# Modulation sums of a diffusion block: from column sums on TensorE to accumulating VectorE operations, with the first projection done block by block

## The reference, cut to what matters

```python
D_MODEL, SEQ, DEPTH, MOD_CHUNKS, SGU_WIDTH, N_MIXERS = 1024, 256, 2, 6, 2048, 3
for i in range(DEPTH):                      # layer 0: gMLP mixer, layer 1: pooling mixer
    mod_lat = split((silu(c) @ ada_w[i] + ada_b[i])[:, None, :], MOD_CHUNKS, axis=-1)   # ada_w[i]: 1024 x 6144
    h_lat = rmsnorm(x_lat, norm1_g[i]) * (1 + mod_lat[1]) + mod_lat[0]
    y_lat = mixer(h_lat)                    # layer 0: z = gelu(h @ w_in); v half normed, mixed over tokens, times u; @ w_out
    x_lat = x_lat + mod_lat[2] * y_lat
    f_in = rmsnorm(x_lat, norm2_g[i]) * (1 + mod_lat[4]) + mod_lat[3]
    x_lat = x_lat + mod_lat[5] * peer(f_in) # product-key expert retrieval over 16,384 experts, tables u and v
out = rmsnorm(x_lat, final_gain)
```

## Time and profile before

| | |
|---|---|
| timed runs | 1875.08, 1877.49, 1878.11 us; median 1877.49 |
| the profiled execution: span from first to last instruction | 1874.9 us |
| median of the timed runs less this span | 2.6 us |
| TensorE busy | 1853.5 us, 99% |
| VectorE busy | 1530.4 us, 82% |
| ScalarE busy | 956.6 us, 51% |
| GpSimd busy | 409.0 us, 22% |
| moved by DMA | 376.38 MB, mean 201 GB/s |

### The profile page before, as it was taken

One profiled execution on the slowest core, in us unless ns is written; L12 is line 12 of the kernel. 1 busy time (PEld: TensorE's weight loads), 2 busy tenths in 40 slices (PEclk: granted clock), 3 DMA queues, 4 the chain that ended last, 5 costly groups with the idle time before them and its releaser, 6 DMA issues.

```text
span 1874.9 us, 35845 instructions
## 1 busy us (share of the span) xinstructions
PE 1853.5 (99%) x11924; PEld 1599.7 (85%) x11924; DVE 1530.4 (82%) x2739; ACT 956.6 (51%) x1588; POOL 409.0 (22%) x197
## 2 busy tenths in 40 slices
PE   7999999999999999999999999999999999999998
PEld 6899998888888888888889998888888888888887
DVE  7785689978988888888887588997998888885555
ACT  3644455655555544445455445565555544445454
POOL 1015578970000000000001258895000000000000
PEclk9999999999999999999999999999999999999999
DMA  9956455556645555578874445556654555555554
GB/s 363 331 204 215 146 171 188 184 185 218 209 167 169 178 170 177 170 284 319 327 280 165 140 160 188 182 188 202 208 207 160 173 173 177 169 175 191 193 190 134
DMA packets 104180, 376.38 MB, mean 201 GB/s; under 512 B 12464, under 2 KB 12464, under 8 KB 103856
## 3 DMA queue, kind: packets, MB, share of 16 engines
q1 hardware_dynamic: 103680, 373.43, 58.6%
q0 software_dynamic: 432, 2.10, 0.3%
HBM read 374.43 MB, written 1.05 MB: 200 GB/s over the span
## 4 chain that ended last, share of the span: by engine, by line
PE 93%; DVE 3%; DMA 2%; ACT 1%; SPq 1%; issue 0%; DVEq 0%; ACTq 0%
PE ring L1708 22%; PE O L1766 13%; PE O L1768 12%; PE O L1767 12%; PE ring L1710 11%; PE ring L1409 3%; PE ring L1410 3%; PE ring L1411 3%; PE ring L1680 3%; PE ring L1701 2%; DMA raw<-in_u 1%; PE O L1701 1%; PE ring L1682 1%; DMA raw<-in_w_in 1%; PE O L1512 1%; PE O L1555 1%
## 5 line engine op out<-in xcount | busy, mean ns | idle before, releaser
L489 ACT ACTIVATE wH<-raw 128x1024 fp32r<-128x1024 f32 x606 | 643.3, 1062 | 833.6 <-DMA raw<-in_v 366.0
L1708 PE MATMUL ring<-hX,wH 128*128 128x512 f32 x1984 | 703.6, 398 | 0.0
L807 DVE TENSOR_TENSOR wL<-raw,wH 128x1024 fp32r<-128x1024 f32 x384 | 470.2, 1224 | 178.7 <-ACT wH L489 175.4
L1710 PE MATMUL ring<-hX,wL 128*128 128x256 f32 x1984 | 554.8, 280 | 0.0
L1708 PEld LDWEIGHTS ring<-hX,wH 128*128 128x128 f32 x1984 | 372.4, 188 | 86.0 <-issue 0.5
L1766 PE MATMUL O<-wH,gateH 128*128 128x512 f32 x1024 | 405.3, 396 | 0.0
L1768 PE MATMUL O<-wH,gateL 128*128 128x512 f32 x1024 | 399.5, 390 | 0.0
L1767 PE MATMUL O<-wL,gateH 128*128 128x512 f32 x1024 | 398.3, 389 | 0.0
L1710 PEld LDWEIGHTS ring<-hX,wL 128*128 128x128 f32 x1984 | 374.4, 189 | 0.0
L452 POOL TENSOR_TENSOR wL<-raw,wH 128x1024 fp32r<-128x1024 f32 x128 | 318.3, 2493 | 53.0 <-ACT wH L489 52.0
L1768 PEld LDWEIGHTS O<-wH,gateL 128*128 128x128 f32 x1024 | 192.2, 188 | 41.2
(11 more groups left out here) (205 smaller groups left out, 2353.7 us busy)
## 6 DMA issues: line engine op xcount, KB each, us to landing
raw<-in_u SPq DMA_DIRECT2D x256, 512.0 KB, 3.3
raw<-in_v SPq DMA_DIRECT2D x256, 512.0 KB, 3.3
ada_v<-in_ada SPq DMA_DIRECT2D x40, 512.0 KB, 4.5
raw<-in_w_in SPq DMA_DIRECT2D x32, 512.0 KB, 4.6
raw<-in_w_q SPq DMA_DIRECT2D x30, 512.0 KB, 3.3
ada_s<-in_ada SPq DMA_DIRECT2D x20, 512.0 KB, 5.2
ada_f<-in_ada SPq DMA_DIRECT2D x16, 512.0 KB, 9.9
raw<-in_w_out SPq DMA_DIRECT2D x16, 512.0 KB, 3.3
```

The source lines that it names most:

```text
L489: nc.scalar.activation(wH[s % RAW][:, :], (place or raw[s % RAW])[:, :], ACT.Copy).then_inc(s_h, 1)
L807: nc.vector.tensor_tensor(wL[s % RAW][:, :], raw[s % RAW][:, :], wH[s % RAW][:, :].bitcast(fp32), ALU.subtract).then_inc(s_low, 1)
L1708: mm(bank[:, :], wH[s][:, k * P:k * P + P], hX[:, k, :, :].rearrange("p two t -> p (two t)"), start=(k == 0), stop=False)
L1710: ins = mm(bank[:, 0:T], wL[s][:, k * P:k * P + P], hH[:, k, :], start=False, stop=(k == KT - 1))
```

## The change

- The host now gives `ada_w` transposed: an ada tile holds 128 output columns on the partitions and all 1,024 rows along the free side. Tile m gives `mod[:, m]` in one VectorE operation: tile times the condition row, with `accum_out` taking the sum along the free side. The row (silu(c) on every partition, 128 x 1024) is made once by 8 matmuls of a broadcast column of csT against the identity into PSUM banks O[2] and O[3], and ScalarE copies it to SBUF as `cond`. In front and in w_out the operation reads the row from PSUM (`O23`, refilled by ScalarE ahead of w_out), elsewhere from SBUF.
- All `modulations` matmuls of TensorE go. In the second norms, and in layer 0's last norm, keep_clock matmuls stand where they stood.
- Front: SyncE loads XT first, then for each pair of k blocks four ada tiles (two of chunk 1, two of chunk 0) mixed with three gate tiles. VectorE sums the two tiles of block k, makes gs and shift for that block, and scales and shifts the block of XT (normed beforehand into `sq`). TensorE takes each block as it comes, in groups 0 to 2 (1,536 columns, six banks), and does group 3 behind them in the last two banks. GpSimd makes the low parts of these twelve tiles in halves, VectorE those of the last four.
- w_out: the low part of all 16 tiles is made by GpSimd, whole.
- Ada tiles: none in w_v beyond the sixteen of the front, 12 loads in w_u (8 of them summed there), 12 loads and 16 sums in w_out (OUT_ADA says how many before each low part's old place: 1, 1, 1, 1, 2, 1, 2, 1, 1, 1, 1, 1, 1, 1, 0, 0); u and v as before, the v loop of VectorE written out.

```diff
@@ SyncE
+            sp.dma_start(XT[:, :, :], xt_d).then_inc(s_x, 16)
+            for g in range(4):
+                if g == 0:
+                    load(stream_dram["w_v", 0], 0, 0, 0, first=True)
+                load_front(4 * g)
+                load_front(4 * g + 1)
+                if g == 0:
+                    load(stream_dram["w_v", 0], 0, 0, 1, first=True)
+                else:
+                    load_gate(3 * g)
+                    load_gate(3 * g + 1)
+                load_front(4 * g + 2)
+                load_front(4 * g + 3)
+                load_gate(3 * g + 2)
+            for t in range(BLOCK_TILES, 16):
+                load_gate(t)
             for dst, src in small_loads:
                 sp.dma_start(dst, src).then_inc(s_small, 16)
...
                 load(stream_dram["w_u", 0], W_U, t // 4, t % 4)
-                if t < 8:
-                    load_ada(ada_s, m)
+                if t < 8 or t > 11:
+                    load_ada(ada_m, m)
                     m += 1
...
                 load(stream_dram["w_out", 0], W_OUT, t // 4, t % 4)
-                if t in ADA_W_OUT:
-                    if t == ADA_W_OUT[0]:
-                        sp.wait_ge(s_gf, SGU_FT)
-                    load_ada(ada_o, m)
+                if 2 < t < 15:
+                    load_ada(ada_m, m)
                     m += 1
@@ GpSimd
-                    low_second(W_OUT, 0, 0, W_OUT + 1)
+                    for t in range(BLOCK_TILES):
+                        front_low(t)
+                    low_out(0, 0, W_OUT + 1)
@@ ScalarE, ahead of w_out
                     gated_high(15, 16)
                     act.wait_ge(s_small, SMALL)
+                    act.wait_ge(s_sv, SGU_FT)
+                    for x in range(2):
+                        nc.scalar.activation(O[2 + x][:, :], cond[:, x * HALF:x * HALF + HALF], ACT.Copy).then_inc(s_filled, 1)
@@ VectorE
+            def add_ada(tile, at):
+                nc.vector.scalar_tensor_tensor(tile[:, :], tile[:, :], 1.0, cond[:, :], ALU.mult, ALU.mult,
+                                               accum_out=mod[:, at:at + 1]).then_inc(s_acc, 1)
+            for k in range(KT):
+                ada_front(2 * k)
+                if k == 0:
                     inverse_root(0)
+                else:
+                    front_rest(k - 1)
+                dve.wait_ge(s_acc, 2 * k + 1)
+                step(nc.vector.scalar_tensor_tensor(gs[:, 0, k:k + 1], modcol(0, 1, k, 1), adab[:, KT + k:KT + k + 1],
+                                                    n1[:, k:k + 1], ALU.add, ALU.mult))
+                ada_front(2 * k + 1)
+                if k == 0:
+                    dve.wait_ge(s_x, 16)
+                    dve.wait_ge(s_rstd, 1)
+                    for j in range(KT):
+                        last = step(nc.vector.tensor_tensor(sq[:, j, :], XT[:, j, :], ring[3][:, 0:T], ALU.mult))
+                    after(last)
+                dve.wait_ge(s_acc, 2 * k + 2)
+                after(step(nc.vector.tensor_tensor(modcol(0, 0, k, 1), modcol(0, 0, k, 1), adab[:, k:k + 1], ALU.add)))
+                nc.vector.tensor_scalar(sq[:, k, :], sq[:, k, :], gs[:, 0, k:k + 1], modcol(0, 0, k, 1), ALU.mult, ALU.add)\
+                    .then_inc(s_xn, 1)
...
                     gated_low(15)
+                    dve.wait_ge(s_filled, 2)
                     for j in range(KT):
                         for s in range(2):
-                            if j or s:
-                                ahead(W_OUT, j // 2, 2 * (j % 2) + s)
+                            for _ in range(OUT_ADA[2 * j + s]):
+                                ada_tile(ada_m, m, psum=True)
@@ TensorE
+            def gate_block(g, s, kk):
+                k = 2 * s + kk
+                if g == 0:
+                    pe.wait_ge(s_hH, k + 1)
+                n = BLOCK_GROUPS * s + g if g < BLOCK_GROUPS else BLOCK_TILES + s
+                if g < BLOCK_GROUPS:
+                    pe.wait_ge(s_first_l, 2 * n + kk + 1)
+                elif kk == 0:
+                    pe.wait_ge(s_l0, 4 * s + 4)
...
+                    for s in range(4):
+                        gate_block(0, s, 0)
+                        if s == 0:
+                            pe.wait_ge(s_xn, 1)
+                        gate_block(1, s, 0)
+                        gate_block(0, s, 1)
+                        gate_block(1, s, 1)
+                        gate_block(2, s, 0)
+                        gate_block(2, s, 1)
+                    pe.wait_ge(s_acc, ADA_FRONT)
+                    pe.wait_ge(s_cond, 2)
+                    for s in range(4):
+                        gate_block(3, s, 0)
+                        gate_block(3, s, 1)
```

More of the change, by code:

```diff
@@ L108, in build @@
             selK = sb("selK", [P, 2, T, 2], bf16, at=one)
-        shared = sb("shared", [P, 6 * T])
+        with ExitStack() as one:
+            iota = sb("iota", [P, KEYS], at=one)
+        shared = sb("shared", [P, 5 * T])
         with ExitStack() as one:
@@ L132, in build @@
         inv = sb("inv", [P, TT])
-        ones = sb("ones", [P, 1])
-        ones_b = sb("ones_b", [P, 1], bf16)
+        cond = sb("cond", [P, D])
         selG = sb("selG", [P, T, 2, 2], fp16)
@@ L850, in modulations @@
+            def modulations(lo_chunk, hi_chunk, norms, unit=None):
+                lo, hi = lo_chunk * KT, hi_chunk * KT
+                dve.wait_ge(s_acc, hi)
+                last = step(nc.vector.tensor_tensor(mod[:, lo:hi], mod[:, lo:hi], adab[:, lo:hi], ALU.add))
                 after(last)
@@ L950, in _ @@
+            front_rest(KT - 1)
+            for t in range(BLOCK_TILES, 16):
+                front_low(t)
+            low_first(W_U, 0, 0)
+            low_first(W_U, 0, 1)
             for layer in range(LAYERS):
@@ L1504, in keep_clock @@
                     mm((ring[3] if bank is None else bank)[:, 0:P], mean_w[:, :], ident[:, :], start=True, stop=True)
-            def modulations(sums, lo, hi, summed, bank, signal=True, blocks=range(KT)):
-                pe.wait_ge(s_acc, summed)
-                for x in range(lo, hi):
-                    for j in blocks:
-                        at = KT * (x - lo) + j
-                        ins = mm(bank[:, at:at + P], sums[:, x, j * P:j * P + P], ones[:, :].to_broadcast([P, P]),
-                                 start=True, stop=True)
-                if signal:
-                    ins.then_inc(s_modp, 1)
             def mix_tile(f):
@@ L1558, in scores @@
                         ins.then_inc(s_sc, 1)
-            pe.wait_ge(s_const, 6)
-            pe.wait_ge(s_acc, 4)
-            keep_clock(12)
-            modulations(acc_f, 0, 1, KT, O[3])
+            pe.wait_ge(s_const, 5)
+            pe.wait_ge(s_silu, 1)
+            for k in range(KT):
+                ins = mm(O[2 + k // 4][:, k % 4 * P:k % 4 * P + P], csT[:, k:k + 1].to_broadcast([P, P]), ident[:, :],
+                         start=True, stop=True)
+                if k % 4 == 3:
+                    ins.then_inc(s_row, 1)
+            keep_clock(6)
             for j in range(KT):
@@ L1656, in _ @@
                 mean(n, KT - 2)
-                shift, x, summed = ((acc_s, 1, ADA_U0), (acc_v, 3, ADA_U1))[layer]
-                pe.wait_ge(s_mod, (4, 9)[layer])
-                modulations(shift, x, x + 1, summed, O[3], signal=False, blocks=range(KT // 2))
+                if layer == 0:
+                    pe.wait_ge(s_acc, ADA_U0)
+                keep_clock(4, O[3])
                 mean(n, KT - 1)
-                modulations(shift, x, x + 1, summed, O[3], blocks=range(KT // 2, KT))
+                keep_clock(4, O[3])
                 spread(n)
@@ L1796, in _ @@
                         pe.wait_ge(s_oc_a, (TT + 1) * layer + TT)
-                    if j == 6 and layer == 0:
-                        pe.wait_ge(s_mod, 7)
                     if j == 4:
```

345 lines of the change are left out of this document (135 added, 210 removed).

## The result

The changed kernel takes **1882.2 us** (median of 9 runs, 1878.8 to 1888.8), the kernel before in the same series 1877.3 (9 runs, 1874.7 to 1878.2). The ratio is 1.0033, 95% interval 1.002 to 1.0045: **slower by a third of a per cent**, where 0.6% faster was forecast. Its runs also spread over 10 us, three times as wide as before.

The account below looks back on a forecast made before the run. TensorE, busy 99% of the span, was taken as the bound. Front -6.0, up tiles +0.8, matmuls removed -12.1, w_out stall +5.4, u stages +0.3 gave -11.6 us: 1877.5 to 1865.9, range 1857 to 1875 (forecast's own 1861 to 1870).

Parts of the forecast that it names:

- What bounds the kernel: Whole kernel: TensorE, busy 99% of the span, waits only in the first 32 us, 11.6 us for sums, next longest 0.5.
- The sums' price: VectorE's accumulating sums: 1.28 us as now, 0.1 of it overlapped, plus 0.17 for reading out the sum: 1.35.
- (D): Rival on VectorE's sums: accumulation takes two passes, 1.07 us more a sum, so 1897 us in all; chance 0.08.
- The front: Start to the up half: gate half ends at 71.4 against 77.4, 6.0 us gained, between 0 and 11.
- the ring: Front: four raw buffers and SyncE's in-order queue make turns of 11.3 us, bounds 9.95 and 13, setting the pace.
- sum, shift and scale 2.75: End of the front: VectorE's 2.75 us after the last ada tile lands, part of 19.7 us to the gate half's end.
- I count nothing for it and leave it to the upper end: Front: TensorE's slower matmuls after gaps, 12 us a turn instead of 8.35, put at no cost.
- 5.4 us lost: w_out: TensorE waits for the fifth tile's low part, ready at S + 16.7, wanted at S + 11.3; S is w_out's start.
- The remainder ends at S + 7.3: w_out: last gated remainder, held by a 2.49 us GpSimd instruction, ends 7.3 us after S, the stage's start.
- The stall comes once: w_out: tile 5 is low at S + 19.1, before tile 4 ends (19.5), so no second stall; S is w_out's start.
- Matmuls removed: Seven column-sum chunks leave TensorE's stream at 1.86 us each, 13.0; 12.1 us gained, bounds 9 and 13.
- two at the end of v: End of the v stage: two of the seven removed column-sum chunks, counted at 1.86 us each.

Follow-up runs that it names:

- e11: Changed kernel with zero-adding matmuls filling TensorE's gaps in front and 8 more keep_clock matmuls ahead of the first block: 1883.9 us, ratio 1.0034.
- e4: Changed kernel with SyncE in front issuing ada tiles 6 to 11 ahead of gate tile 4 and 12 to 15 ahead of gate tile 7: 1878.5 us, ratio 1.0009.
- e16: e15 with the six small loads behind w_u's tile 1 instead of ahead of its tile 0: 1870.3 us, ratio 0.9956.
- e3: Changed kernel with ScalarE copying otok before it splits the third p_in tile at the end of layer 0's v stage: 1881.4 us, ratio 1.0018.
- e8: Changed kernel with 16 keep_clock matmuls where the two chunks' column sums had stood before the last v tile: 1885.9 us, ratio 1.0052.
- e15: Changed kernel with the edits of e4 and e3, w_out low parts by halves and its ada loads one a tile from tile 5: 1866.4 us, ratio 0.9946.
- e12: e15's edits on the changed kernel, plus e11's zero-adding fillers and the small loads ahead of gate tile 4: 1871.4 us, ratio 0.9967.
- e2: Changed kernel with w_out's low parts by halves on VectorE and GpSimd as before, SyncE's order as changed: 1880.8 us, ratio 1.0018.
- e1: Changed kernel with w_out's twelve ada tiles loaded two at a time behind tiles 7 to 12: 1883.8 us, ratio 1.0025.

## Why the prediction was wrong

**What bounds the kernel: right, with a slip.** Beside the 11.6 us TensorE's longest wait was not 0.5 us but one of 1.1, in front too, and it does wait behind the front: four times in the first u stage (0.4 us at most, 1.0 in all) and 0.6 us in the last norm. The sum doesn't use them.

**The sums' price: right.** 1.21 us and a read of 0.08 against 1.28 and 0.17; (D) is refuted. The Trainium skill's Vector Engine (DVE) Microarchitecture Reference, in Points that are easy to get wrong, says that this form with two non-bf16 SBUF sources halves throughput; the trace disagrees, with 1,214 ns for 1,024 elements from SBUF and the same from PSUM.

**The front: the ring right, its tail and the clock not.** A turn was 11.7 us for 11.3, and the first tile of the last pair of ada tiles was there at 52.3, where the last one was forecast for 51.7. Of the 3.5 us that were missing in the profiled execution most lie in the tail: "sum, shift and scale 2.75" has one sum, where behind the pair's first tile came its sum (from 52.34), a remainder, gs held for 1.23 us, and the second sum, so that ScalarE began the last hH at 56.90 and not at 54.5. That is 2.4 of the 3.5. For the median the step that failed is "I count nothing for it and leave it to the upper end", said of TensorE's slower rate after gaps: in five of six executions with this order of transfers stretches at the 1.2 GHz level appear in front, and the up half starts between 74.9 and 82.0. The range of the front was given as 66.5 to 77, and four of the six are above it. Its ends don't follow from the turns alone, either: two turns of 13 us in place of 11.3 give 74.8, and two of 9.95 give 68.7. How much of these delays is the clock and how much the transfers isn't separated by the trace: e11 held the clock at 1.00 with this order and ended at 78.5 with its fillers in the way, e4 changed the order alone and ended at 71.3 with the clock at 1.00. Shown is that the order of transfers moves the front by some 6 us (means 78.1, and 71.9 without e16, whose small loads no longer stand ahead of w_u's), and that the lower clock is then rarer.

**The w_out stall: the mechanism right, its price not.** The wait came at the fifth tile, released by GpSimd, and the sum's chain is the one written down. "5.4 us lost" measured 7.2: TensorE wanted the low part 13.2 us into the stage (forecast 11.3) and went on at 20.4 (forecast 16.7). Two terms made the chain late. "The remainder ends at S + 7.3" was 9.4, because the longer GpSimd instructions also held two remainders ahead and, behind them, the split of tile 3. The forecast named this case ("7 if more of the remainders ahead are held by the longer GpSimd instructions") and left it out of the sum. And tile 4 took 5.5 us to land, not 4.2. (The other 0.3 us are small steps.) TensorE's later want is mostly a wait of its own for the same remainder, 1.5 us, which the sum doesn't have: by S + 7.3 the remainder would have been in time for TensorE at S + 7.9. "The stall comes once" left out that the clock is at half for 3.8 us behind it, 1.9 us; and 0.9 us is a wait for a square. 7.2 + 0.2 (a second wait for GpSimd) + 1.5 + 1.9 + 0.9 = 11.7; less the 1.9 of the removed column sum that is 9.8 of the measured 10.8. The last microsecond wasn't placed.

The same w_out code ran in five profiled executions (the changed kernel, e3, e4, e8, e11). Their longest wait for GpSimd was 7.2, 6.0, 4.8, 4.7 and 5.9 us, 5.7 on the average, so that 5.4 was a fair size for the stall and 7.2 the largest of the five. Yet the stage took 62.5 to 65.2 us in all of them, 8.1 to 10.8 above before where 3.5 was forecast. What every one of them has and the sum has not is TensorE's wait for the last remainder (1.4 to 2.2 us) and a stretch at a granted clock of 0.50.

**Matmuls removed: five of seven, one of these in part.** In w_u, w_out and p_in they gave about what was counted (w_u's 1.9 less 1.0 of waiting for a late up tile, where 0.8 was forecast; another 0.4 stands ahead of the first up tile, in front; w_out's is taken as counted in the sum above). In the two u stages the ledger has -2.8 and -1.7 for -1.7 each, 0.7 of the extra in layer 0 being shorter waits for the grids' inputs, 0.3 us for 1.0. Over the twelve executions it is -1.9 and -0.6 on the average, against the single one of before: the first is borne out, the second only in part, within a scatter of 4 us. The two at the end of v gave nothing: "two at the end of v" was costed by its own duration, and what TensorE would wait for next wasn't asked, though the forecast did ask it in layer 1. e8 shows this, and e3 that 1.6 us come once the copies are let through.

**The balance.** Front 3.5, w_out 7.3, v 4.4 and w_u 0.4 worse, u, layer 0, 1.1 better: 14.5 of the 14.7 us between the forecast -11.6 and the measured +3.1 of the profiled pair. With the three faults mended, e15 ran at 1866.4, half a microsecond from the forecast. But that is another kernel, and its agreement is luck in good part: its w_out has no stall and is 3.1 us better than forecast, its v stage gives 1.7 and not 3.7 us, and layer 1's w_q and u stages give nothing of 1.7. The medians are further apart than the profiled pair, 16.3 us between 1865.9 and 1882.2, since the changed kernel's profiled execution was a fast one.

## What to carry to other kernels

When matmuls are taken out of a stream that never waits, ask at each place what the next instruction needs and when it is ready: two of seven here had only covered a wait. Behind a wait of a few microseconds put the slower clock in the sum, half the length of the stretch that runs at 0.50: here 1.9 us behind a wait of 7.2, and 2.9 behind one of 3.9. When an engine's instructions get longer, ask which instructions of its neighbour they will hold, all of them and not only the last. And where one execution of a stage is compared with one other, look first how far executions of the same code lie apart. In a queue that is served in order, move the loads whose buffers are free ahead of one that waits for its buffer; here that was worth 4.5 us (ratio 1.0009 for 1.0033). Large loads that nobody needs yet, put ahead of a tile that is soon needed, made TensorE wait 3.4 us for it (e12).

## What was not expected of the hardware

- A one-column VectorE operation on SBUF (128 x 1) takes 0.16 to 0.21 us and 1.23 to 1.25 beside a GpSimd half tile; a 128 x 256 remainder takes 2.38 us beside a whole tile of 2.37. Both lengths follow GpSimd's instruction, and not the size of VectorE's own. The sums, with an operand in PSUM, stay at 1.21 beside it.
- The granted clock fell to 0.50 behind a wait of 3.4 us (e12), of 3.86 (e2), of 7.2 (after), and also behind one of 2.0 (e4, 0.50 from 137 to 139) and one of 2.1 (e1; mean 0.79 for 144 to 152), but not behind one of 1.55 (after, 1.00 from 138 to 142). Nor does the longer wait bring the longer stretch: 5.9 us behind the 3.86, 3.8 behind the 7.2. Behind the 2.75 us wait at the end of v it read 0.69 in the five microseconds around it. In front it fell in some executions and not in others of the same code.
- The filled front (e11) repeats within 1.4 us, the changed kernel's runs spread over 10. Only the profiled execution of each kernel shows its front, so that the spread comes from the front's clock is argued and not shown. Fillers alone don't settle it: e12 has them and spreads over 6.5 us, e15 has none and spreads over 2.8.
